# Seven units of work change places in a two-block transformer kernel on one core

## What is computed

```python
h = x
for i in range(DEPTH):                       # DEPTH = 2
    a = rms_norm_2(h, norm_attn[i])
    u = a @ w_in[i]
    ...                                      # split into the inputs of four mixers
    o_a = nsa_attention(...)                 # three attentions, gated
    o_b = diff_attention(...)                # softmax 1 - lambda * softmax 2, then a norm
    o_c = gla_mixer(...)                     # a gated recurrence, then a norm and a gate
    o_d = hgrn2_mixer(...)                   # another, likewise
    h = h + concatenate([o_a, o_b, o_c, o_d]) @ w_out[i]
    c = rms_norm_2(h, norm_ffn[i])
    h = h + (swiglu(c, ...) if i % 2 == 0 else moe_swiglu(c, ...))   # 8 experts, top 2
    gate = sigmoid(rms_norm_2(h, ple_norm[i]) @ ple_w_gate[i])
    h = h + (p[i] @ ple_w_proj[i]) * gate
```

## Time and profile before

| | us |
|---|---|
| median of 3 runs | 2643.92 (2643.88 to 2646.43) |
| the profiled execution | 2646.02 |
| its span | 2644.5 |
| TensorE busy | 2550.8 (96%) |
| VectorE busy | 642.5 (24%) |
| ScalarE busy | 488.0 (18%) |
| GpSimd busy | 134.3 (5%) |
| mean granted clock | 0.972 of full |

### The profile page before, as it was taken

One profiled execution on the slowest core, in us unless ns is written; L12 is line 12 of the kernel. 1 busy time (PEld: TensorE's weight loads), 2 busy tenths in 40 slices (PEclk: granted clock), 3 DMA queues, 4 the chain that ended last, 5 costly groups with the idle time before them and its releaser, 6 DMA issues. The chain is left out here.

```text
span 2644.5 us, 47407 instructions
## 1 busy us (share of the span) xinstructions
PE 2550.8 (96%) x21427; PEld 1429.2 (54%) x21427; DVE 642.5 (24%) x1352; ACT 488.0 (18%) x830; POOL 134.3 (5%) x331
## 2 busy tenths in 40 slices
PE   9999999999999988999999988999999999999999
PEld 8666557766554774444445764353444535353444
DVE  3534523433533532000024432000101001010002
ACT  1521321421322432001013430100000000000001
POOL 4011000011000210000001200000000000000000
PEclk9999999998999988999999888999999999999999
DMA  7421333421335412444446114999999999999992
GB/s 244 132 76 55 127 117 119 152 74 56 112 120 130 135 49 90 153 145 141 151 133 174 63 43 160 375 363 380 355 385 346 377 364 369 373 369 371 361 375 89
DMA packets 192349, 542.29 MB, mean 205 GB/s; under 512 B 29168, under 2 KB 57232, under 8 KB 192144
## 3 DMA queue, kind: packets, MB, share of 16 engines
q1 hardware_dynamic: 178848, 536.95, 56.3%
q10 hardware_dynamic: 12992, 1.22, 0.4%
q0 software_dynamic: 304, 1.05, 0.1%
HBM read 538.12 MB, written 1.05 MB: 204 GB/s over the span
## 5 line engine op out<-in xcount | busy, mean ns | idle before, releaser
L399 PE MATMUL psum<-ring,hT 128*128 128x512 f32 (+3 forms) x1632 | 685.8, 578 | 13.1 <-ACT area L746 7.0
L399 PEld LDWEIGHTS psum<-ring,hT 128*128 128x128 f32 x1632 | 309.0, 197 | 348.1 <-issue 322.9
L2604 PE MATMUL psum<-ring,area 128*32 128x448 f32 x4608 | 439.5, 539 | 1.7 <-DVE area L2780 1.1
L2604 PEld LDWEIGHTS psum<-ring,area 128*32 128x32 f32 x4608 | 149.9, 110 | 283.8 <-issue 279.9
L632 PE MATMUL psum<-hT,ring 128*128 128x256 f32 x768 | 169.5, 384 | 0.0
L632 PEld LDWEIGHTS psum<-hT,ring 128*128 128x128 f32 x768 | 148.1, 193 | 21.4 <-issue 1.0
L2623 PE MATMUL psum<-area 128*32 128x256 f32 x2688 | 149.8, 380 | 2.0 <-ACT area L2753 2.0
L2623 PE MATMUL psum<-ring,area 128*32 128x256 f32 x2688 | 151.5, 380 | 0.0
L2604 PE MATMUL psum<-area 128*32 128x448 f32 x1536 | 147.3, 539 | 0.0
L2623 PEld LDWEIGHTS psum<-area 128*32 128x32 f32 x2688 | 85.7, 110 | 60.2 <-ACT area L2753 3.9
L2623 PEld LDWEIGHTS psum<-ring,area 128*32 128x32 f32 x2688 | 84.9, 110 | 57.1 <-issue 2.9
(11 more groups left out here) (526 smaller groups left out, 2354.0 us busy)
## 6 DMA issues: line engine op xcount, KB each, us to landing
ring<-in_w_in_dram SPq DMA_DIRECT2D x92, 1024.0 KB, 5.1
ring<-in_moe_w_gate_dram SPq DMA_DIRECT2D x96, 896.0 KB, 6.6
ring<-in_moe_w_up_dram SPq DMA_DIRECT2D x96, 896.0 KB, 8.2
area<-in_moe_w_down_dram SPq DMA_DIRECT2D x112, 512.0 KB, 7.4
ring<-in_moe_w_down_dram SPq DMA_DIRECT2D x112, 512.0 KB, 6.9
area<-in_moe_w_gate_dram SPq DMA_DIRECT2D x32, 896.0 KB, 7.4
area<-in_moe_w_up_dram SPq DMA_DIRECT2D x32, 896.0 KB, 8.3
ring<-in_w_out_dram SPq DMA_DIRECT2D x16, 1024.0 KB, 5.1
```

The lines of the kernel that those rows point to most:

```text
L399: last = nc.tensor.matmul(acc(g)[:, t, 0:d["n"]], lhs(kk, t), w[:, k, :], start=kk == 0, stop=kk == d["nk"] - 1)
L2604: last = nc.tensor.matmul(PS[32 * j:32 * j + 32, 3 * p + b, 0:PIECE], XG[:, k, 32 * b:32 * b + 32], expert_slot(j0 + j // 2, GROUP * (j % ...
```

## The change

Seven edits, none of which changes what is computed:

1. The first norm: the squares of the second half of the tokens go from ScalarE to VectorE.
2. `MIXER_PLAN`: three moves, the same in both layers. A fill quarter goes ahead of "exp 1" and "scores 2" (it stood behind them); recurrence unit 12 goes ahead of a fill quarter and of "turn 3"; a fill quarter goes ahead of "turn 4" (three quarters before it and one behind, where there were two and two).
3. `post_act`: `root_table` behind the early squares.
4. The end of the first layer: each unit of the product signals for itself, and VectorE multiplies and adds the right half of the columns in two pieces, one for each half of the tokens. The other waits on this semaphore count one more.
5. `pass_dve`: only expert 0's comparisons stand ahead of the gather; those of the other seven come behind the shares.

```diff
         def squared_by_vector(n):
 
-            return () if n == 0 else ((0, 1), (1, 1)) if n == 8 else ((1, 1),)
+            return ((0, 1), (1, 1)) if n in (0, 8) else ((1, 1),)
...
             for half, t in squared_by_vector(n):
+                if n == 0:
+                    x_half(s.eng, n, half)
                 s.do(row_squares(nc.vector, X, half, t, SS))
...
-        MIXER_PLAN = "cgfencfgcfngcfvgcfagfccgfacgfdafcaadfgdeaafgafagfaagfaaafgaaffagfafagafaavgffaffapgpvgpp"
+        MIXER_PLAN = "cgfencfgcfngcfvgcfagfccgfacgfdafcaadfgdefaagafagfaagfaaafgaafgfafafagafaavgfffafapgpvgpp"
...
                     .then_inc(signal("m_osq_early"), 1), "m_osq_early")
+            root_table(s)
             yield
...
-                ple_unit(pe, L, 1, 0, 6)
+                ple_unit(pe, L, 1, 0, 6).then_inc(sem("ple_unit"), 1)
                 ple_unit(pe, L, 1, 1, 7).then_inc(sem("weights_used"), 1)
...
                 s.eng.wait_ge(sem("gemm_out_act"), evacuated(g1)[1])
+                s.eng.wait_ge(sem("ple_unit"), 2)
+                s.do(nc.vector.tensor_tensor(TMP[:, 0, :], SGP[:, 0, 512:1024], PS[:, 6, :], ALU.mult))
+                s.do(nc.vector.tensor_tensor(X[:, 0, 512:1024], X[:, 0, 512:1024], TMP[:, 0, :], ALU.add))
                 s.eng.wait_ge(sem("weights_used"), used(TILES[group("pp", L)[1]]["first"]))
-                add(X[:, :, 512:1024], TMP, SGP[:, :, 512:1024], PS[:, 6:8, :], "x_updated")
+                add(X[:, 1, 512:1024], TMP[:, 1, :], SGP[:, 1, 512:1024], PS[:, 7, :], "x_updated")
...
-            for t in range(T):
-                ins = nc.vector.tensor_tensor(PALL[:, t, 0:NE, :], bc(IOTA.unsqueeze(1), [P, NE, CAP]),
-                                              bc(SLOT[:, t].unsqueeze(2), [P, NE, CAP]), ALU.is_equal)
-                if t == 0:
-                    s.do(ins)
-                else:
-                    s.after(ins.then_inc(ms("placed"), 1), "moe_placed")
+
+            def chosen(t, e0, e1):
+                return nc.vector.tensor_tensor(PALL[:, t, e0:e1, :], bc(IOTA.unsqueeze(1), [P, e1 - e0, CAP]),
+                                               bc(SLOT[:, t, e0:e1].unsqueeze(2), [P, e1 - e0, CAP]), ALU.is_equal)
+
+            s.do(chosen(0, 0, NE if r else 1))
+            s.after(chosen(1, 0, NE if r else 1).then_inc(ms("placed"), 1), "moe_placed")
             if r:
                 clear_dve()
             else:
                 shares_dve(s)
+                for t in range(T):
+                    s.do(chosen(t, 1, NE))
```

More of the change, by code:

```diff
@@ L2374, in ple_act @@
             else:
-                s.eng.wait_ge(sem("ple_unit"), 3)
+                s.eng.wait_ge(sem("ple_unit"), 4)
                 s.after(nc.scalar.activation(PR[:, 0, 512:1024], PS[:, 3, :], ACT.Copy).then_inc(sem("ple_out_act"), 1), "ple_out_act")
@@ L2382, in ple_act @@
             else:
-                s.eng.wait_ge(sem("ple_unit"), 4)
+                s.eng.wait_ge(sem("ple_unit"), 5)
                 s.after(nc.scalar.activation(SGP[:, 0, 512:1024], PS[:, 2, :], ACT.Sigmoid).then_inc(sem("ple_out_act"), 1), "ple_out_act")
@@ L2406, in ple_dve @@
                 for c in range(2):
-                    s.eng.wait_ge(sem("ple_unit"), 5 + c)
+                    s.eng.wait_ge(sem("ple_unit"), 6 + c)
                     cols = slice(512 + 256 * c, 768 + 256 * c)
@@ L2766, in pass_act @@
             if not r:
-                act.wait_ge(sem("ple_unit"), 2)
+                act.wait_ge(sem("ple_unit"), 3)
                 s.after(nc.scalar.activation(PR[:, 0, 0:512], PS[:, 3, :], ACT.Copy).then_inc(sem("ple_out_act"), 1), "ple_out_act")
```

## The result

| | before | changed |
|---|---|---|
| median, us | 2645.07 (2643.88 to 2647.22, 5 runs) | 2619.24 (2615.63 to 2624.43, 5 runs) |
| the profiled execution, us | 2646.02 | 2621.88 |
| mean granted clock in it | 0.972 | 0.978 |

A forecast was written before the change was run, and what follows sets the result against it. TensorE, busy 2550.8 of 2644.5 us, was taken as the bound, leaving 93.7 us of waits; seven terms (0.3 + 2.5 + 2.5 + 3.5 + 2.6 + 1.1 + 1.4) made 13.9 us, so 2643.9 became 2630.0 us, range 2621 to 2639.

The forecast's parts named there:

- The clock comes back too: Mixing stages: with gaps nearly filled, half-clock runs return to full clock, some 5 us more, 2625 us; chance 0.2.
- Start: First norm: two of four squares to VectorE end TensorE's 0.28 us wait for the reciprocal; gain 0.3 us.
- A quarter ahead of scores 2: Both mixing layers: the moved quarter fills TensorE's 1.26 us wait for ScalarE's copy; gain 2.5 us, bounds 0 and 5.4.
- Unit 12: Mixing: the unit fills the quarter's wait for L1510, 2.33 us in layer one, 0.75 in two; gain 2.5, bounds 0 and 5.5.
- A quarter ahead of turn 4: Both layers: the quarter uses about 1.75 of TensorE's 2.76 us wait for L1949; gain 3.5 us, bounds 1.7 and 3.9.
- The table: After mixing, both layers: the 1.28 us square-root table load moves off the path to the root; gain 2.6 us.
- End of the first layer: VectorE's last product L2391 starts behind the first unit and ends at 1385.2, not 1386.3; gain 1.1 us.
- The gather: First expert: comparisons on 96 columns instead of 768 let the gather start at 1631.6, not 1633.0; gain 1.4 us.
- Waits passed on: Mixing moves: filled gaps reopen at the next unit, only the other four edits' 5.4 us stay, 2638.5 us; chance 0.12.
- Slower by the clock: Mixing, where dense quarters are taken away: narrow products let TensorE fall to 1.2 GHz, 2649 us or more; chance 0.03.

The follow-up runs named there:

- the first quarter alone: The kernel before with only the fill quarter moved ahead of scores 2, in both layers: 2638.20 us, ratio 0.9969.
- the quarters alone: The kernel before with only the two fill quarters moved, ahead of scores 2 and of turn 4, recurrence unit 12 where it was: 2628.49 us, ratio 0.9947.
- the order alone: The kernel before with only the three moves of `MIXER_PLAN`, in both layers: 2635.30 us, ratio 0.9963; again 2628.72 us, ratio 0.993.

## Why the prediction was wrong

The step that failed is "The clock comes back too" as a rival. The sum had a term for each wait and none for the clock, which was put beside it as another way for things to go, at 5 us and a chance of 0.2. It was no alternative to the sum but a further term of it, and it measured 8.3 us in the whole kernel and 12.6 in the mixing stages. Its mechanism was right, though its own price (2625) would have been too small as well, with the two quarters it named: 3.42 became 1.99 at 961.13, and two in 5.3 became three in 5.40 at 977.56. Its argument against was one gap of 2.76 us without a fall behind it; one gap that does nothing says little about what six gaps in the same stage do together. The Trainium skill's rule that was cited for it (TensorE: Matmul & The Clock Gate, A second HAM failure mode) is borne out here: brief idling between groups of matmuls goes with falls of the clock, and with the gaps filled the clock of the two stages rose from 0.83 and 0.84 to 0.93 and 0.90, or to 0.91 and 0.89 where only unread matmuls filled them.

The waits came to 10.6 of 11.1 us in the mixing stages, and that is luck in part, since two terms missed in opposite ways, as the list shows. The sum's own high bounds add up to 20.2 us, not to the 19 that the prediction gives; 24 to 26 lie beyond either.

Term by term:

- **Start, 0.3: nothing.** The reciprocal is there at 7.90, but TensorE transposes parameters until the scales at 9.19. The wait of 0.28 is gone and nothing that could be measured follows.
- **A quarter ahead of scores 2, 2.5: the wait went, as said.** No L1870 waits for L1660 any more. Turn 1 starts at 932.19 without a wait. But the margin of turn 1 was there only because the changed kernel still has 6.8 us at half clock just ahead, in both layers. In the first quarter alone TensorE comes sooner, and 1.8 of the 2.5 came back as a wait for the exponentials. What that quarter gives alone is mostly clock.
- **Unit 12, 2.5: right against the kernel before (2.3 alone), undersized beside the other edits (3.8), because of the second layer.** There 0.75 was read in front of the quarter behind a run at half clock; with the clock back it is 2.33, and the unit fills both. The bound of 5.5 held this. In the second layer turn 3 now waits 0.5 us for its probabilities, as the prediction said that it would.
- **A quarter ahead of turn 4, 3.5: right.** The waits of the turns for L1949 went from 5.5 to 2.1 with the quarters alone.
- **The table, 2.6: right.** L450's wait for VectorE's last scaling (L2217, now L2220) went from 4.1 to 1.6. The load starts 0.01 us behind the squares, so there is no drain here either.
- **End of the first layer, 1.1: right** (1.8 to 0.7). **The gather, 1.4: right** (2.5 to 1.1), but the run at half clock that it lies in is now 20.5 us long where it was 17.1, so the stretch from the routed norm to the next became only 0.5 shorter.
- **Waits passed on** did not come in the whole change, where the windows' idle time fell by 10.6 of the 11.1 forecast. In the first quarter alone this rival was right: 2.5 us of waits went and as much came back.
- **Slower by the clock** did not come either, but something of its kind did, elsewhere: in the order alone, half-clock time outside the mixing windows is 122 us against 89 before (146.8 and 150.2 in all, less 25 and 61.5 within). Some of that is chance between executions, the stretch ahead of the mixing above all. The part behind it stands in both profiles of the order alone. Why it appears there with some plans and not with others was not settled. It goes with no edit at those places.

## What to carry to other kernels

Where a tuned kernel shows runs at half clock next to short waits of TensorE, price a filled wait twice: its own length, and the half-clock time around it at about a third of its length (0.34 us for each us here). Read a wait that follows a run at half clock as a lower bound, since a late engine waits less, and expect it at its full length once the clock is back. Before you add up waits, ask which of them hold only while TensorE is late: filling one can turn another up. And compare such variants by several sets of runs with the clock beside each: two medians of five runs of the same kernel lay 6.6 us apart here, and two single profiles 9.6 us in a stretch that no edit touched.

## What the runs showed of the hardware

Matmuls whose result nobody reads can make a kernel faster. 23 of them around the routed norm, the router and the gather, 12 in each of two more norms and 8 at each mixing's end took the changed kernel from 2622 to 2610 us and its profiled clock from 0.975 to 0.984, though TensorE then works more. More of them is not better: with 74 in place of the 23 and none elsewhere, half-clock time fell as well (95.7 us in all against 116.3 to 130.0) and the kernel gained nothing; with the 23 alone it gained nothing measurable either. And the clock is not local in its cause: with the order alone, both profiles have runs at half clock of 6.8 us in a stage behind the edit whose instructions it did not touch, and which the kernel before lacks. Runs ahead of any edit come and go between executions by themselves.
